# A fused two-block kernel on one Trainium2 core: the first stage (modulation, norms, filter sines) rebuilt

## The reference, cut to what matters

```python
mod_x = (jax.nn.silu(c) @ w_mod[layer] + b_mod[layer])[:, None, :]      # c: (1, 1024)
mod_c = jax.nn.silu(c_ctx) @ w_mod[layer] + b_mod[layer]                # c_ctx: (1024,)
sh_m, sc_m, gt_m, sh_f, sc_f, gt_f = jnp.split(mod_x, N_MOD, axis=-1)
hx = modulate(rms_norm(x, g_pre_mix[layer]), sh_m, sc_m)                # x: 512 tokens
hc = modulate(rms_norm(ctx, g_pre_mix[layer]), csh_m, csc_m)            # ctx: 256 tokens
...
h = jnp.sin(fr * (pos @ _f32(f_w1) + _f32(f_b1)))                       # filter network, 512 x 64
h = jnp.sin(fr * (h @ _f32(f_w2) + _f32(f_b2)))
h = jnp.sin(fr * (h @ _f32(f_w3) + _f32(f_b3)))
```

## Time and profile before

| | |
|---|---|
| median of 3 runs | 1572.43 us |
| the profiled execution: its own time | 1570.12 us |
| its span in the trace | 1568.3 us, 16986 instructions |
| busy: TensorE matmul, VectorE, ScalarE, GpSimd | 1460.6, 942.6, 523.2, 186.0 us |
| on the chain that ended last | TensorE 84%, VectorE 9%, ScalarE 2%, GpSimd 2% |
| read from HBM, written | 162.96 MB, 2.10 MB |

### The profile page before, as it was taken

The page is one execution under the profiler, slowest core; times in us unless marked ns, Lnnn a source line. Parts: engine busy times, 40 slices in busy tenths (PEclk is TensorE's granted clock), DMA queues, the critical chain, the costliest instruction groups (busy, mean ns, idle before and its releaser), DMA issues.

```text
span 1568.3 us, 16986 instructions
## 1 busy us (share of the span) xinstructions
PE 1460.6 (93%) x6192; PEld 1124.3 (72%) x6192; DVE 942.6 (60%) x1203; ACT 523.2 (33%) x728; POOL 186.0 (12%) x169
## 2 busy tenths in 40 slices
PE   8599999999969999999999899986597999999996
PEld 6588887555747888888884488854485888888885
DVE  6842477777356666663234676559726888887222
ACT  1423353444353232332223522320335333333221
POOL 4401520000200000000110020027220000000000
PEclk9999999999989999999999999997798999999998
DMA  7322231133306666664421022300021232223221
GB/s 272 121 87 70 88 93 41 55 107 134 127 35 225 216 214 218 212 240 141 162 73 40 14 88 99 121 14 1 27 81 67 83 105 94 94 95 128 93 74 53
DMA packets 44366, 168.62 MB, mean 108 GB/s; under 512 B 5499, under 2 KB 6075, under 8 KB 43036
## 3 DMA queue, kind: packets, MB, share of 16 engines
q1 hardware_dynamic: 42908, 165.08, 31.0%
q0 software_dynamic: 1408, 2.89, 0.7%
HBM read 162.96 MB, written 2.10 MB: 105 GB/s over the span
## 4 chain that ended last, share of the span: by engine, by line
PE 84%; DVE 9%; ACT 2%; POOL 2%; issue 1%; DMA 1%; SPq 0%; DVEq 0%; ACTq 0%; POOLq 0%
PE PS L578 67%; PE PS L863 3%; PE PS L966 2%; DVE tb L1663 2%; PE PS L826 2%; PE PS L825 1%; PE PS L1060 1%; DVE H L1663 1%; PE PS L646 1%; DMA wraw<-w_mod_a 1%; POOL acc L1572 1%; DVE zpD L2209 1%; DVE wsp L567 1%; PE PS L850 1%; PE PS L636 1%
## 5 line engine op out<-in xcount | busy, mean ns | idle before, releaser
L578 PE MATMUL PS<-H,wsp 128*128 128x512 f32 x3600 | 835.5, 393 | 27.5 <-DVE H L1663 17.9
L578 PEld LDWEIGHTS PS<-H,wsp 128*128 128x128 f32 x3600 | 678.7, 189 | 178.9 <-issue 17.9
L567 DVE TENSOR_TENSOR wsp<-wraw,wsp 128x1024 fp32r<-128x1024 f32 (+1 forms) x182 | 237.7, 1307 | 437.4 <-ACT wsp L561 436.9
L561 ACT ACTIVATE wsp<-wraw 128x1024 fp32r<-128x1024 f32 (+1 forms) x182 | 202.7, 1115 | 531.5 <-PE PS L578 529.4
L578 PE MATMUL PS<-hid,wsp 128*128 128x512 f32 x1056 | 240.0, 389 | 0.0
L578 PEld LDWEIGHTS PS<-hid,wsp 128*128 128x128 f32 x1056 | 198.2, 188 | 41.8 <-issue 0.8
L1663 DVE SCALAR_TENSOR_TENSOR cva<-PS,dert,cva 128x441 f32<-128x441 f32 (+2 forms) x176 | 122.2, 694 | 5.5
L1569 POOL COPY acc<-sqb 128x512 f32<-128x512 f32 x5 | 5.1, 1012 | 774.0 <-ACT sqb L1382 287.4
L1572 POOL TENSOR_TENSOR acc<-acc,sqb 128x512 f32<-128x512 f32 x31 | 52.5, 1693 | 201.4 <-ACT sqb L1547 82.6
L1891 DVE CUSTOM_DVE_ANT_0 sink<-mring,crow_t,colt 128x1024 bf16<-128x1024 f32 x56 | 71.7, 1280 | 0.4
L1060 PE MATMUL PS<-invt,KS 128*128 128x256 f32 x128 | 32.9, 425 | 22.2 <-DVE row L2246 22.2
(11 more groups left out here) (284 smaller groups left out, 1403.6 us busy)
## 6 DMA issues: line engine op xcount, KB each, us to landing
mring<-mod_c SPq DMA_DIRECT2D x56, 512.0 KB, 4.5
wraw<-w_ffn_in SPq DMA_DIRECT2D x44, 512.0 KB, 3.3
wraw<-w_up SPq DMA_DIRECT2D x44, 512.0 KB, 3.3
wraw<-w_mod_b SPq DMA_DIRECT2D x24, 512.0 KB, 3.4
wraw<-w_hy_in SPq DMA_DIRECT2D x24, 512.0 KB, 3.3
wraw<-w_w_in SPq DMA_DIRECT2D x22, 512.0 KB, 3.4
wraw<-w_ffn_out SPq DMA_DIRECT2D x16, 704.0 KB, 4.1
wraw<-w_down SPq DMA_DIRECT2D x16, 704.0 KB, 4.1
```

What stands on the lines that cost most here:

```text
L561: nc.scalar.activation(wsp[:, o % 2, 0, 0:n], wraw[:, g % RAW, 0:n], ACT.Copy).then_inc(w_hi, 1)
L567: nc.vector.tensor_tensor(wsp[:, o % 2, 1, 0:n], wraw[:, g % RAW, 0:n], wsp[:, o % 2, 0, 0:n].bitcast(F32), ALU.subtract).then_inc(w_lo, 1)
L578: mm = nc.tensor.matmul(psum, wsp[:, o % 2, a, wk * P:(wk + 1) * P], h[:, b, kt, :], start=first and kt == kts[0] and (a, b) == (0, 0), st ...
```

## The change

- All 16 units of the first stage get a place of their own: four in the slots, twelve in `mfirst`, where H and other tiles lie later. No load of the stage waits for a slot.
- The loads come in a new order (`MOD_ORDER`), and between them the matrices, x and ctx; two rows of conditions (silu of c and c_ctx, 0.5 MB each, broadcast to all partitions) come second and third, the filter's inputs last.
- Units 0 to 5 are multiplied on TensorE as before, units 6 to 15 as rows on VectorE (two reductions each). Nothing of it is left on GpSimd, and the folds are gone.
- The squares of both norms are summed on TensorE, tile by tile, as for k = 3 and 5.
- The sine layers move into the projection: matmuls after w_in 1, 3 and 5 on TensorE (and into bank 4 of PSUM), arguments at steps 2, 4 and 6 on VectorE, sines at steps 2, 4 and 6 on ScalarE. The silu of c at step 12 is gone.

```diff
-PHASES = [("mod_a", 16, U1, False), ("w_in", 22, U1, True), ("mod_b", MOD_B, U1, False),
+MOD_ORDER = (0, 6, 7, 1, 8, 9, 2, 10, 11, 3, 12, 13, 4, 14, 5, 15)
+MOD_ON_PE = 6
+PHASES = [("mod_a", 4, U1, False), ("w_in", 22, U1, True), ("mod_b", MOD_B, U1, False),
...
+        mfirst = [sb(f"mfirst{i}", o_h + 4 * K * i, [P, U1]) for i in range(8)] + \
+                 [sb(f"mfirst{i}", o_r + 24 * K + 4 * K * (i - 8), [P, U1]) for i in range(8, 12)]
...
-        PE_SUMS = (3, 5)
+        PE_SUMS = (0, 1, 3, 5)
...
-                    elif ordinal in OFF_PE:
-                        k = OFF_PE.index(ordinal)
-                        sp.wait_ge(a_pr[0], k + 1 if k < 3 else 2 * k - 1)
-                        if k < 3:
-                            sp.wait_ge(a_pr[1], k + 1)
-                    elif ordinal < 16:
-                        sp.wait_ge(mod_done, ON_PE.index(ordinal) + 1)
+                    elif name == "w_in":
+                        m = MOD_ORDER[ordinal]
+                        if m < MOD_ON_PE:
+                            sp.wait_ge(mod_done, m + 1)
+                        else:
+                            sp.wait_ge(a_md, 2 * (m - MOD_ON_PE + 1))
                     else:
-                        sp.wait_ge(m_rd, ordinal - 16 + 1)
+                        sp.wait_ge(m_rd, ordinal - RAW + 1)
...
-            sp.dma_start(colt[:, :], cols).then_inc(s_small, 16)
+            sp.dma_start(colt[:, :], cols).then_inc(s_cols, 16)
+            for v in range(2):
+                sp.dma_start(crow_t[:, v, :], crow[:, 2 * v]).then_inc(s_crow, 16)
+
+            def load_first(x):
+
+                if x < RAW:
+                    load("mod_a", x, x, w["mod_a"][x])
+                else:
+                    sp.dma_start(mfirst[x - RAW][:, :], mod_x[x - RAW]).then_inc(mfirst_on[x - RAW], 16)
+
+            load_first(0)
+            load_first(1)
+            for j, m in enumerate((ones, bones, swap, ident)):
+                sp.dma_start(m[:, :], mats[j]).then_inc(s_small, 16)
+            load_first(2)
+            for k0 in (0, KT // 2):
+                sp.dma_start(X[:, k0:k0 + KT // 2, :], xT[:, k0:k0 + KT // 2]).then_inc(s_x, 16)
+            for x in range(3, 7):
+                load_first(x)
+            sp.dma_start(Xc[:, :, :], ctxT).then_inc(s_xc, 16)
+            for x in range(7, 16):
+                load_first(x)
             sp.dma_start(posb[:, :], posT).then_inc(s_feat, 16)
             sp.dma_start(fwb[:, :, :], fw).then_inc(s_feat, 16)
...
-                    sp.dma_start(crow_t[:, 0, :], crow[:, 0]).then_inc(s_crow, 16)
...
+                x = MOD_ORDER.index(m)
+                first_landed(pe, x)
                 for kt in range(KT):
-                    mm = nc.tensor.matmul(PS[:, 7, 2 * m:2 * m + 2], wraw[:, m % RAW, kt * P:(kt + 1) * P],
+                    mm = nc.tensor.matmul(PS[:, 7, 2 * m:2 * m + 2], first_unit(x)[:, kt * P:(kt + 1) * P],
                                           dert[:, DER["silu_c"] + 3 * kt:DER["silu_c"] + 3 * kt + 2],
                                           start=kt == 0, stop=kt == KT - 1)
                 mm.then_inc(mod_done, 1)
...
             def squares_total(k, kts=range(KT)):
 
-                pe.wait_ge(n_rt, k)
+                if k >= 2:
+                    pe.wait_ge(n_rt, k)
+                bank, n = (5, LC) if k == 1 else (6, L)
                 for kt in kts:
                     q = k * KT + kt
                     pe.wait_ge(n_sq, q + 1)
-                    nc.tensor.matmul(PS[:, 6, :], ones[:, :], sqb[:, q % 2, :], start=kt == 0,
+                    nc.tensor.matmul(PS[:, bank, 0:n], ones[:, :], sqb[:, q % 2, 0:n], start=kt == 0,
                                      stop=kt == KT - 1).then_inc(n_acc, 1)
...
-            pe.wait_ge(s_feat, 32)
-            pe.wait_ge(s_small, 80)
-            filter_layer(0)
             pe.wait_ge(silu_c, 1)
-            for n, m in enumerate(ON_PE):
-                modulation(m)
-                if n in (2, 5):
-                    filter_layer((n + 1) // 3)
-            pe.wait_ge(f_arg, 3)
-            total(0)
-            total(1)
-            for which in range(2):
-                for i in range(len(OFF_PE)):
-
-                    pe.wait_ge(a_sum[0 if which == 0 or i >= 3 else 1],
-                               i + 1 if i < 3 else 2 * i - 2 + which)
-                    c = 2 * OFF_PE[i] + which
-                    nc.tensor.matmul(PS[:, 7, c:c + 1], asum[:, 2 * i + which, :], der("one"), start=True,
-                                     stop=True).then_inc(mod_done, 1)
+            modulation(0)
+            pe.wait_ge(s_small, 64)
+            modulation(1)
+            squares_total(0)
+            modulation(2)
+            modulation(3)
+            squares_total(1)
+            modulation(4)
+            modulation(5)
...
+                if n in (1, 3, 5):
+                    if n == 1:
+                        pe.wait_ge(s_feat, 32)
+                    filter_layer(n // 2)
...
-            act.wait_ge(s_small, 80)
+            act.wait_ge(s_cols, 16)
             SC.activation(der("silu_c", 0, 3 * KT), col("c", 0, 3 * KT), ACT.Silu).then_inc(silu_c, 1)
+            act.wait_ge(s_crow, 32)
+            for v in range(2):
+                SC.activation(crow_t[:, v, :], crow_t[:, v, :], ACT.Silu).then_inc(crow_on, 1)
             SC.activation(der("lg_f", 0, 8), col("dec_f", 0, 8), ACT.Exp).then_inc(m_lg, 1)
             SC.activation(der("lg_b", 0, 8), col("dec_b", 0, 8), ACT.Exp).then_inc(m_lg, 1)
             SC.activation(der("lg_p", 0, 8), col("dec_p", 0, 8), ACT.Exp).then_inc(m_lg, 1)
-            for l in range(3):
-                act.wait_ge(f_arg, l + 1)
-                if l:
-                    act.wait_ge(f_mm, l + 1)
-                SC.activation((fh if l < 2 else feat)[:, :], fa[:, :], ACT.Sin).then_inc(f_sin, 1)
...
-            act.wait_ge(n_ss, 1)
+            act.wait_ge(n_acc, KT)
             SC.activation(rtmp[:, :], PS[:, 6, :], ACT.Ln, bias=col("eps")).then_inc(n_rt, 1)
-            act.wait_ge(n_ss, 2)
+            act.wait_ge(n_acc, 2 * KT)
             SC.activation(accc[:, :], PS[:, 5, 0:LC], ACT.Ln, bias=col("eps")).then_inc(n_rt, 1)
...
+            def filter_sine(l):
+
+                act.wait_ge(f_arg, l + 1)
+                SC.activation((fh if l < 2 else feat)[:, :], fa[:, :], ACT.Sin).then_inc(f_sin, 1)
...
+                    if n in (2, 4):
+                        filter_sine(n // 2 - 1)
...
-                if n == 12:
-                    act.wait_ge(s_crow, 16)
-                    SC.activation(crow_t[:, 0, :], crow_t[:, 0, :], ACT.Silu).then_inc(crow_on, 1)
+                if n == 6:
+                    filter_sine(2)
...
-                        if k >= 2:
+                        if k > 2:
                             pool.wait_ge(n_ss, totals(k - 1))
...
-            def mod_a_product(i):
-
-                if i:
-                    pool.wait_ge(a_sum[1], i)
-                mod_a_multiply(pool, PL, 1, i, 1)
-                pool.wait_ge(a_pr[1], i + 1)
-                pm = aprod[:, 1, :]
-                own(PL.tensor_tensor(pm[:, 0:512], pm[:, 0:512], pm[:, 512:1024], ALU.add))
-                own(PL.tensor_tensor(pm[:, 0:256], pm[:, 0:256], pm[:, 256:512], ALU.add))
-                PL.tensor_tensor(asum[:, 2 * i + 1, :], pm[:, 0:128], pm[:, 128:256], ALU.add).then_inc(a_sum[1], 1)
-
-            pool.wait_ge(silu_c, 1)
-            for i in range(3):
-                mod_a_product(i)
-            sums(0)
-            sums(1, LC)
...
-            def mod_a_product(i, which):
-
-                if count[0]:
-                    dve.wait_ge(a_sum[0], count[0])
-                count[0] += 1
-                mod_a_multiply(dve, VE, 0, i, which)
-                dve.wait_ge(a_pr[0], count[0])
-                VE.tensor_reduce(asum[:, 2 * i + which, :], aprod[:, 0, :].rearrange("p (k n) -> p n k", n=P),
-                                 mybir.AxisListType.X, ALU.add).then_inc(a_sum[0], 1)
-
-            dve.wait_ge(s_small, 80)
-            dve.wait_ge(silu_c, 1)
-            for l in range(3):
-                mod_a_product(l, 0)
+            def first_modulations(m):
+
+                x = MOD_ORDER.index(m)
+                first_landed(dve, x)
+                for which in range(2):
+                    done = 2 * (m - MOD_ON_PE) + which
+                    if done:
+                        dve.wait_ge(a_md, done)
+                    VE.tensor_tensor_reduce(sink[:, :], first_unit(x), crow_t[:, which, :], 1.0,
+                                            col("b_mod", 2 * m + which), ALU.mult, ALU.add,
+                                            dert[:, DER["mod"] + 2 * m + which:DER["mod"] + 2 * m + which + 1]
+                                            ).then_inc(a_md, 1)
+
+            def filter_argument(l):
+
...
-                own(VE.tensor_scalar(fa[:, :], PS[0:HYF, 6, :], colt[0:HYF, COL[b]:COL[b] + 1],
```

(56 more changed lines are left out.)

31 lines of the change are left out of this document (4 added, 27 removed).

## The result

The changed kernel takes 1554.39 us (median of 4 runs, 1552.29 to 1557.84) against 1571.81 us: ratio 0.9893, interval 0.9872 to 0.9914, so 1.1% less. The forecast was 1557.5 us in a range of 1551 to 1566.5. Its profiled execution took 1553.57 us with a span of 1551.6, 16.7 less than before. One execution of one later variant ("before, both") took 2948 us, nearly twice as long as any other; it stands in no median and no ratio.

The account below looks back on a forecast made before the run. TensorE bounds most of the span, but early on it waits for the modulation columns. Columns 17.9 us earlier, less 2.9 for sine layers, give -15.0 on 1570.12: 1555.1, as a median 1557.5 us, range 1551 to 1566.5.

Parts of the forecast that it names:

- VectorE ends: First stage: VectorE finishes its last reduction at 45.3 us, at 2.66 us a unit and 2.87 us of small operations.
- columns: End of first stage: VectorE takes the modulation columns out of PSUM at 49.1 us instead of 67.0, 17.9 us earlier.
- three layers: Projection: three sine layers, each two records of 512 columns on TensorE, 1.0 us each, add 2.9 us on the path.
- from the profiled execution to the median: Whole kernel: the median of runs lies 2.3 us above the profiled execution, as in the kernel before.
- What ends the stage: First stage: TensorE, not VectorE, is the late engine, ending at 48.9 us against VectorE's 45.3.
- Transfers: First stage loads: no wait for a slot, 0.373 MB per us after 20 us, the last unit landing at 39.4 us.
- Cover: Projection: VectorE's arguments and ScalarE's sines finish before TensorE needs them, covered by 2.5 us.
- a step over 10.8 us: Projection: sign that would show the prediction wrong, one step taking longer than 10.8 us.
- VectorE as the end of the stage: First stage: rival with TensorE at the high level, ending at 44.4; columns at 45.5, 18.6 us saved, 1554; chance 0.22.
- The low level throughout: First stage: rival with TensorE at the low clock level to 57.9 us, 6.1 us saved, 1566.3; chance 0.12.
- stalls by the sine layers: Projection: rival in which the sine layers stall it by another 5 to 8 us, 1564; chance 0.08.
- by the transfers: First stage: rival in which transfers end the stage, columns at 68.1, 4.0 us slower, 1576.4; chance 0.03.

Follow-up runs that it names:

- before, both: Kernel before with the totals on TensorE and the sine layers in the projection, keeping four slots, ten units on TensorE and the folds: 1567.0 us, ratio 0.9974.
- the other execution: The changed kernel run once more, unaltered, with a second trace: 1553.9 us, ratio 0.9891.

## Why the prediction was right

By its own steps, forecast and measured in the changed kernel's trace:

| step | forecast | measured |
|---|---|---|
| unit 1 starts | 19.7 | 19.04 |
| unit 1; total of x | 3.5; 9.7 | 3.55; 9.37 |
| units 2 and 3 | 5.0 | 3.47 |
| total of ctx | 6.0 | 5.61 (35.42 to 41.03) |
| units 4 and 5 | 5.0 | 3.99 |
| TensorE ends | 48.9 | 45.02 |
| VectorE ends | 45.3 | 43.44 |
| columns | 49.1 | 45.12 |
| three layers | +2.9 | +3.6 |
| from the profiled execution to the median | +2.3 | +0.8 |

- **What ends the stage** was right: TensorE's written order, with VectorE 1.6 us ahead of it. The sum was 3.9 us too high there, 2.5 of it in the units. I had put them between the levels, a third of the way up from the high one; here they ran at the high one but for unit 5's last 1.2 us. In the other execution (4.4 and 4.86 us) they were nearer my 5.0. One number for it is wrong to begin with.
- **Transfers** were mis-sized on the safe side: 413 GB/s from 20 to 27 us are 0.41 MB per us, a unit in 1.27 us; my 0.373 was the mean of a stretch whose parts ran from 298 to 444 GB/s.
- **VectorE**: the reductions cost a little more than I said (2.74 us a unit from 24.23 to 43.44: two reductions start 1.32 us apart within a unit and 1.44 across units), the small operations half, 1.48 for 2.87 us. The row I priced them by the earlier trace rows had GpSimd working beside it. That is the step that the prediction lacked as a mechanism: it counted GpSimd's work as gone from the chain and never as gone from beside VectorE. VectorE's end came out only 1.9 us late because the errors were small and of both signs: 0.9 from the landing of unit 8, 1.4 from the small operations and 0.2 from unit 8's reductions, less 0.6 for the seven units behind.
- **The layers** were 0.7 us short: besides 1.00 us for its records each makes the products behind it 0.18 us longer, which I read as their first loads left in the open. Cover held: no engine waits for a sine in the projection. One of my own signs of being wrong was met all the same: a step over 10.8 us. The steps with a layer take 10.88 us (72.74 to 83.62) and 10.90 (93.32 to 104.22), of which 9.7 is the step of before, 1.0 the layer and 0.18 the longer products. I had set the limit so near my own 10.7 that this 0.18 alone crosses it; it tells of a cost too low, not of a stall.
- **The rivals**: VectorE as the end of the stage was near (1.7 us), and its time, 1554, is what was measured, but not its mechanism. Its premise on the level was nearer than mine: from the end of the total of x on TensorE took 13.1 us, where the rival had 11.5 and I had 16.0. The low level throughout did not come; nor did stalls by the sine layers or by the transfers.
- The time is right in part by errors that cancel, which is luck: 4.0 us more gained in the stage, against 0.7 more paid for the layers, 1.35 us lost to the clock at the start of attention, and 0.2 between the columns and the first product (5.5 us for 5.3). That leaves the profiled execution 1.5 us below its 1555.1. The other 1.5 of the 3.1 us between 1557.5 and 1554.4 is the step from that execution to the median: I took over the 2.3 us of the kernel before, and here it is 0.8.
- The reading of the Trainium skill's rule on the throttle ("TensorE: Matmul & The Clock Gate", the section on the HAM clock gate) stands halfway. The granted clock fell to 0.50 at 37 us though TensorE had been busy almost without a gap (9.92 of 10 us), against the bare rule; but for some us after a total the units have the high level, which I counted only in part.

## What to carry to other kernels

Price a stage by engine and take the latest, but ask of every row you price by what ran beside it: an operation of VectorE with two inputs in SBUF cost 1.3 to 1.6 times as much here with GpSimd adding, and operations on 8 columns over four times. What a part of a change is worth depends on what stands beside it: the sums on TensorE brought the columns 4.0 us earlier alone, 5.0 later on top of the moved sine layers, and 5.9 earlier in the changed kernel. So test parts in pairs, too. And where TensorE has work of few columns, put it right behind dense work.

## What was not expected of the hardware

- GpSimd's additions slow VectorE's two-input reductions from 1284 to 2052 ns although nothing waits for them: 8.2 us of a kernel of 1554. Seven operations on 8 columns, with one tile as input, are slowed more, 5.3 us for 1.2.
- The same program has its clock low for 3 or nearly 7 us within the first stage's totals and units, and low or not at the start of attention (235 us), from one execution to the next. Each moves the time by 1 to 2.5 us, which is as much as several of the edits tested gain or lose.
- One queue with no slot to wait for holds 413 GB/s for 7 us (20 to 27), where the same queue before reached 444 for 2.5 us and held 373 over 17.5.
